# GpSimd takes the low halves of one projection, the second layer's S5 parameters are made earlier, and half of the LRU input product is done in split form

## What is computed

```python
h = rms_norm(x, norm_g)
p = h @ w_in                      # u_lru, u_s5, q/k/v of retention, nsa q, nsa k/v, gates, merges
y = [rg_lru(u_lru), s5(u_s5), retention(q, k, v), nsa(q, kv)]      # each 512 wide
merged = sum(sigmoid(merge_b) * ((silu(gate_b) * y_b) @ w_branch[b]) for b in 4 branches)
x = x + merged @ w_out
# S5: dt = exp(log_dt); a = exp(lam * dt) (complex); B and C are scaled by functions of a and lam
```

## Time and profile before

| | us |
|---|---|
| median of 3 runs | 751.04 |
| lowest and highest | 749.69, 751.25 |
| time of the profiled execution | 749.62 |
| its span, first to last instruction | 747.8 |
| TensorE busy | 734.8 |
| VectorE busy | 486.2 |
| ScalarE busy | 421.2 |
| GpSimd busy | 307.4 |

### The profile page before, as it was taken

How to read it: one execution, slowest core, us unless ns; L and a number is a source line. 1 busy time by engine, 2 the same in 40 slices (tenths; PEclk the granted TensorE clock), 3 DMA queues, 4 the chain that set the end, 5 groups by cost and what they waited for, 6 DMA issues and landing times.

```text
span 747.8 us, 14583 instructions
## 1 busy us (share of the span) xinstructions
PE 734.8 (98%) x6014; PEld 623.7 (83%) x6014; DVE 486.2 (65%) x786; ACT 421.2 (56%) x676; POOL 307.4 (41%) x135
## 2 busy tenths in 40 slices
PE   8999999999999999999989999999999999999996
PEld 7888898889888888878888878988898788888785
DVE  5989977675685634535688799767565947153344
ACT  7885635538464655544558664444476345655442
POOL 3000000035977976688100000000647979766750
PEclk9999999999999999999999999999999999999999
DMA  8669637553553655555545875665625456545541
GB/s 261 188 197 272 218 124 226 185 180 114 159 151 115 196 147 144 164 173 167 150 95 169 283 190 172 202 201 187 200 85 169 134 149 175 168 137 170 172 137 56
DMA packets 87009, 126.85 MB, mean 170 GB/s; under 512 B 22072, under 2 KB 32672, under 8 KB 86944
## 3 DMA queue, kind: packets, MB, share of 16 engines
q1 hardware_dynamic: 86624, 125.63, 55.9%
q10 hardware_dynamic: 320, 0.30, 0.1%
HBM read 124.86 MB, written 1.05 MB: 168 GB/s over the span
## 4 chain that ended last, share of the span: by engine, by line
PE 93%; DVE 3%; issue 2%; ACT 1%; DMA 0%; POOL 0%; SPq 0%; POOLq 0%; DVEq 0%; ACTq 0%
PE proj L1745 68%; PE M L1740 5%; PE proj L1782 4%; PE proj L1786 2%; PE proj L1813 2%; PE M L2140 2%; PE M L1942 1%; DVE sc L1556 1%; PE M L1953 1%; PE M L1910 1%; PE proj L1828 1%; PE proj L1844 1%; PE M L2114 1%; PE M L2017 1%; PE M L2109 1%
## 5 line engine op out<-in xcount | busy, mean ns | idle before, releaser
L698 POOL TENSOR_TENSOR w_lo<-raw,w_hi 128x1024 fp32r<-128x1024 f32 x112 | 291.4, 2633 | 391.8 <-ACT w_hi L720 368.7
L720 ACT ACTIVATE w_hi<-raw 128x1024 fp32r<-128x1024 f32 x200 | 206.5, 1054 | 108.8 <-PE proj L1745 64.8
L1745 PE MATMUL proj<-w_hi,h_hi 128*128 128x512 f32 x544 | 216.8, 399 | 0.0
L1745 PE MATMUL proj<-w_hi,h_lo 128*128 128x512 f32 x544 | 212.4, 390 | 0.0
L1745 PE MATMUL proj<-w_lo,h_hi 128*128 128x512 f32 x544 | 212.0, 390 | 0.0
L1745 PEld LDWEIGHTS proj<-w_hi,h_lo 128*128 128x128 f32 x544 | 102.1, 188 | 22.2 <-issue 0.5
L1745 PEld LDWEIGHTS proj<-w_hi,h_hi 128*128 128x128 f32 x544 | 102.2, 188 | 21.8 <-issue 0.9
L1745 PEld LDWEIGHTS proj<-w_lo,h_hi 128*128 128x128 f32 x544 | 102.3, 188 | 20.4 <-issue 0.5
L1329 DVE TENSOR_TENSOR w_lo<-raw,w_hi 128x1024 fp32r<-128x1024 f32 x80 | 95.0, 1221 | 27.0 <-ACT w_hi L720 19.5
L1745 PE MATMUL proj<-w_hi,ys_hi 128*128 128x512 f32 x128 | 51.0, 398 | 0.0
L1745 PE MATMUL proj<-w_hi,ys_lo 128*128 128x512 f32 x128 | 50.0, 391 | 0.0
(11 more groups left out here) (342 smaller groups left out, 1175.7 us busy)
## 6 DMA issues: line engine op xcount, KB each, us to landing
raw<-in_w_in SPq DMA_DIRECT2D x152, 512.0 KB, 4.3
raw<-in_w_branch SPq DMA_DIRECT2D x32, 512.0 KB, 4.0
raw<-in_w_out SPq DMA_DIRECT2D x16, 512.0 KB, 4.1
raw<-in_s_w_glu SPq DMA_DIRECT2D x8, 512.0 KB, 4.8
raw<-in_w_in SPq DMA_DIRECT2D x8, 256.0 KB, 3.0
merged<-in_nsa_ck_w SPq DMA_DIRECT2D x4, 512.0 KB, 6.9
mt<-in_nsa_ck_w SPq DMA_DIRECT2D x4, 512.0 KB, 8.9
merged<-in_nsa_cv_w SPq DMA_DIRECT2D x4, 512.0 KB, 4.6
```

Source lines behind the costliest of these rows:

```text
L698: nc.gpsimd.tensor_tensor(w_lo[:, slot(s, l), 0:n * w], raw[:, u % N_RAW, 0:n * w], w_hi[:, slot(s, l), 0:n * w].bitcast(f32), ALU.subtrac ...
L720: i = nc.scalar.activation(out_, in_, func, **kw)
L1745: last = mm(dst, left[i], right[j], start=start and n == 0, stop=stop and n == 2, skip_group_check=True)
```

## The change

Three things. (1) `nsa_kv` leaves `LO_ON_VECTOR`, so that GpSimd subtracts its four units in each layer. (2) Units 2 and 3 of `u_lru` are no longer native: ScalarE casts them after it has read the `cmp` chunk, VectorE subtracts them between `make_v(0)` and `make_v(1)`, and TensorE multiplies them in split form, as it does for `gate_lru`. The low part of `ret_v` unit 0 comes ahead of `make_v(1)` too. (3) In the first layer all five pieces of parameters of the second are made before the output projection's second half: `expand_dt`, `keep_vectors` and `_a` before `branch("nsa", 0)`, `_e` behind it, `_b`, `_c` and `_d` between `branch("nsa", 1)` and the lo part of the second half of `merged`. TensorE's `turn_vectors` moves from behind the second `blocks_T` to behind `branch_nsa_0`, and ScalarE's exponentials and sines move with it. The second layer no longer has `_c` and `_d` at its start.

```diff
-NATIVE = ("cmp", "u_lru")
+NATIVE_UNITS = [... "cmp" units 0 to 3, "u_lru" units 0 and 1]
-LO_ON_VECTOR = ("u_s5", "ret_v", "nsa_kv", ...
+LO_ON_VECTOR = ("u_s5", "u_lru", "ret_v", ...
...
                     run(bgate[:, :, :], cm[:, :, 256:CMP_W], ACT.Tanh, cmp_read, scale=0.5)
+                    cast_units(UNIT_END[CHUNK["u_lru"]])
                     keep_wT(0, 0)
...
                     cast_room("branch_nsa_0")
+                    if l + 1 < DEPTH:
+                        parameters_exp(l + 1)
...
                             cast_units(UNIT_END[CHUNK["branch_nsa_1"]] + N_SPLIT)
+                            if l + 1 < DEPTH:
+                                parameters_mag(l + 1)
+                                parameters_sin(l + 1)
...
                     make_v(0)
+                    split_lo("u_lru", 2, 3)
+                    split_lo("ret_v", 0)
                     make_v(1)
-                    split_lo("ret_v", 0, 1)
+                    split_lo("ret_v", 1)
...
-                    split_lo("nsa_kv", 0, 1)
                     scan_out(0)
-                    split_lo("nsa_kv", 2, 3)
...
                     lo_of_gated("nsa")
-                    branch("nsa", 0)
-
                     if l + 1 < DEPTH:
                         expand_dt(vector, l + 1)
+                        keep_vectors(vector, l + 1)
+                        parameters_a(l + 1)
+                    branch("nsa", 0)
+                    if l + 1 < DEPTH:
+                        parameters_e(l + 1)
                     for half in range(2):
                         if half:
                             branch("nsa", 1)
+                            if l + 1 < DEPTH:
+                                parameters_b(l + 1)
+                                parameters_c(l + 1)
+                                parameters_d(l + 1)
                         dve.wait_ge(mhi_done, half + 1)
...
                     chunk("branch_nsa_0")
-
+                    if l + 1 < DEPTH:
+                        pe.wait_ge(no_cmp, 1)
+                        turn_vectors(tensor, l + 1)
                     chunk("branch_nsa_1", 0)
                     pe.wait_ge(mt_free, 5)
+                    if l + 1 < DEPTH:
+                        Layer(tensor, l + 1).wait_ge(vec_ready, 1)
                     blocks_T(0, merged[:, 0]).then_inc(mT_done, 1)
...
-                    if l + 1 < DEPTH:
-                        turn_vectors(tensor, l + 1)
                     chunk("out_1a")
```

More of the change, by code:

```diff
@@ L69 @@
 N_SPLIT = 5
-NATIVE = ("cmp", "u_lru")
-SPLIT_UNITS = [u for u in range(NU) if CHUNKS[UNITS[u][0]][0] not in NATIVE]
-LO_ON_VECTOR = ("u_s5", "ret_v", "nsa_kv", "gate_s5", "gate_lru", "merge_s5_0", "merge_s5_1", "ret_q", "ret_k", "nsa_q",
+NATIVE_UNITS = [u for u in range(NU) if (CHUNKS[UNITS[u][0]][0], u - UNIT_END[UNITS[u][0] - 1]) in
+                [("cmp", n) for n in range(4)] + [("u_lru", n) for n in range(2)]]
+SPLIT_UNITS = [u for u in range(NU) if u not in NATIVE_UNITS]
+LO_ON_VECTOR = ("u_s5", "u_lru", "ret_v", "gate_s5", "gate_lru", "merge_s5_0", "merge_s5_1", "ret_q", "ret_k", "nsa_q",
                 "out_0b", "out_1b")
@@ L106 @@
     "dec_ready": 2, "dt_exp": 1, "dt_rows": 1, "evacuated0": 16, "evacuated1": 16, "gate_tanh": 2, "h_done": 2,
-    "hfull_done": 8, "hhi_done": 8, "hi_done": 100, "hidT_done": 2, "hid_arg": 1, "hid_ready": 1, "hid_tanh": 1,
+    "hfull_done": 8, "hhi_done": 8, "hi_done": 102, "hidT_done": 2, "hid_arg": 1, "hid_ready": 1, "hid_tanh": 1,
     "hid_tm_ready": 2, "hlo_done": 8, "kcT_done": 1, "kcT_ready": 1, "kc_ready": 1, "kern_ready": 2, "kp_done": 2,
-    "lam_abs": 1, "lam_exp": 1, "lo_done": 56, "lru_act": 16, "lru_m2": 1, "lru_mm": 1, "lru_sqrt": 1,
+    "lam_abs": 1, "lam_exp": 1, "lo_done": 60, "lru_act": 16, "lru_m2": 1, "lru_mm": 1, "lru_sqrt": 1,
     "mT_done": 2, "mag_arg": 1, "mag_exp": 1, "mhi_done": 2, "mlo_done": 2, "mt_free": 6, "nT_done": 2,
@@ L115 @@
     "v0_ready": 1, "v_ready": 2, "var": 2, "vbd_ready": 1, "vecT": 2, "vec_ready": 1, "vectors_loaded": 208,
-    "vk_ready": 2, "vlo_done": 44, "wT_done": 4, "wT_ready": 4, "w_ready": 2, "wbd_ready": 2, "wl_loaded": 64,
+    "vk_ready": 2, "vlo_done": 42, "wT_done": 4, "wT_ready": 4, "w_ready": 2, "wbd_ready": 2, "wl_loaded": 64,
     "xT_done": 4, "x_half": 3, "x_scaled": 4, "xc_ready": 1, "y_done": 2, "y_ready": 2, "yg_hi": 4, "yg_lo": 4,
@@ L1217, in _ @@
                         vector.wait_ge(const_loaded, 16)
-                    parameters_c(l)
-                    parameters_d(l)
+                        parameters_c(0)
+                        parameters_d(0)
                     v.memset(u_lru[:, :, 0:3], 0.0)
@@ L1674, in _ @@
                     lo_of_gated("nsa")
+                    if l + 1 < DEPTH:
+                        expand_dt(vector, l + 1)
+                        keep_vectors(vector, l + 1)
+                        parameters_a(l + 1)
                     branch("nsa", 0)
                     if l + 1 < DEPTH:
-                        expand_dt(vector, l + 1)
+                        parameters_e(l + 1)
                     for half in range(2):
@@ L1684, in _ @@
                                         flat(h_hi[:, 4 * half:4 * half + 4, :]).bitcast(f32), ALU.subtract).then_inc(mlo_done, 1)
-                    if l + 1 < DEPTH:
-                        split_lo("out_0b", 0)
-                        keep_vectors(vector, l + 1)
-                        split_lo("out_0b", 1)
-                        parameters_a(l + 1)
-                        parameters_e(l + 1)
-                    else:
-                        split_lo("out_0b", 0, 1)
+                    split_lo("out_0b", 0, 1)
                     split_lo("out_1b", 0, 1)
@@ L1706, in _ @@
                                            ALU.mult, ALU.add).then_inc(x_half, 1)
-                    if l + 1 < DEPTH:
-                        parameters_b(l + 1)
-                    else:
+                    if l + 1 == DEPTH:
                         vector.wait_ge(g_loaded, 16)
@@ L1762, in chunk @@
                             _, k0, nk, _ = UNITS[u]
-                            if name in NATIVE:
+                            if u in NATIVE_UNITS:
                                 pe.wait_ge(raw_loaded[u % N_RAW], raw_target[u])
@@ L1787, in chunk @@
                                                       start=st_, stop=sp_, skip_group_check=True)
-                                elif name in ("gate_s5", "gate_lru"):
+                                elif name in ("u_lru", "gate_s5", "gate_lru"):
                                     for m in range(4):
@@ L2197, in _ @@
                     if l + 1 < DEPTH:
-                        Layer(tensor, l + 1).wait_ge(vec_ready, 1)
                         for t in range(TT):
```

3 lines of the change are left out of this document (removed).

## The result

The changed kernel takes **758.94 us** (median of 4 runs, 758.83 to 759.29) against 750.41 us (749.69 to 751.25) for the kernel before on the same chip: a ratio of 1.0121, 95% interval 1.0109 to 1.0133. It is slower, as forecast, but by 8.5 us instead of 4.75, and lies 1.4 us above the range. (The forecast stood on 751.04 us, the median of the three runs of before that were there at the time; with a fourth run it is 750.41.) The profiled execution has a span of 757.0 us, 9.2 more than before.

The account below looks back on a forecast made before the run. TensorE's own list of work was taken to bound the kernel, any new VectorE lateness paid in full. -2.2 + 1.85 + 3.7 + 1.4 = +4.75 us on the median 751.04 gave 755.8 us; range 752.2 to 757.5.

Parts of the forecast that it names:

- Split half of `u_lru`: TensorE's list shortens 1.1 us a layer, 2.2 in all; a 1.85 us stop in layer one, none in layer two.
- Hand-over: End of layer one: `keep_vectors` and a held `_a` delay the pair; `blocks_T` 4.1 us late, 3.7 net of the turn.
- The clears: End of layer one: GpSimd's clears hold VectorE's `_b`, so `out_0b`'s low part is 1.4 us late.
- Rival (a): End of layer one: the clears do not hold VectorE; +3.35 us, 754.4; chance 0.21.
- (b): Hand-over: small one-input operations take no turns with GpSimd; +1.75 us, 753 to 754; chance 0.14.
- (c): Hand-over: no turns there as GpSimd is elsewhere, only the order counts; +0.35 us, 751.4; chance 0.08.
- (d): VectorE reaches `u_lru` in time, the end's hand-over hides, only TensorE's shorter list counts; -2.2 us, 748.9; chance 0.05.
- `nsa_kv` on GpSimd: Both layers: costed at nothing; VectorE's scans lose turns, with some 10 us until TensorE asks for them.
- Rival (e): GpSimd is late with `nsa_kv` or `ret_v` slips, 1 us a layer more; 757.8; chance 0.10.
- Behind the hand-over: From the first `blocks_T` to `out_0b`: `_b` ends at 362.6, `out_0b`'s low part is there at 369.3, 1.4 us late.

Follow-up runs that it names:

- f1: Kernel before with only the second layer's parameters made early, but `keep_vectors` and `_a` behind the first branch pair; 755.36 us, ratio 1.0076.
- e4: The changed kernel with `nsa_kv`'s subtractions back on VectorE, the two other parts kept; 757.63 us, ratio 1.0101.
- g2: The changed kernel with the update of the first half of `x` ahead of the next layer's two input low parts on VectorE; 757.07 us, ratio 1.0089.
- e2: Kernel before with only units 2 and 3 of `u_lru` split; 749.49 us, ratio 0.9999.
- e3: Kernel before with only `nsa_kv`'s subtractions moved to GpSimd; 750.96 us, ratio 1.0014.
- g1: Kernel before with `u_lru` units 2, 3 split, subtracted before `make_v(0)` in layer one, and `nsa_kv` unit 0's low part before the scans; 747.36 us, ratio 0.9961.
- g4: g1 with `nsa_kv`'s four subtractions a layer on GpSimd, none of them ahead of the scans on VectorE; 752.36 us, ratio 1.0035.
- g3: Kernel before with two unused copies of 1024 numbers from PSUM on VectorE ahead of the first branch pair in layer one; 752.38 us, ratio 1.0035.
- f4: Kernel before with three unused copies of 1024 numbers from PSUM on VectorE ahead of the first branch pair in layer one; 754.96 us, ratio 1.0081.
- e1: Kernel before with only the second layer's parameters made early; 756.96 us, ratio 1.0099.

## Why the prediction was right, and where it was wrong

**Split half of `u_lru`: right.** 5.94 us for 5.9. The start is 1.90 us behind that in the earlier trace rows, of which 0.11 come from the start of the program, for 1.85; the bracket shows 1.62 of it. Layer two has no stop. Net +0.72 and -1.16 us for +0.75 and -1.1.

**Hand-over: right in mechanism, 0.5 us too high.** One tiny operation of `_a` was held for a turn, 2.36 us where I had said 2.4. `blocks_T` came 3.69 late for 4.1, and 3.23 net of the turn for 3.7; the distance to `branch_nsa_0` is 6.43 for 6.8.

**The clears: right, though the gap is not to be seen in the changed kernel's own trace.** The clears hold `_b` (f1: 2.95 us, e4: 2.96, changed kernel: 1.73), but one operation and not two. The gap ahead of `out_0b` is 1.41 in e4 and 1.38 in g2. In the changed kernel's trace a lower clock stands in its place, which costs 1.57. Rival (a) falls, and so do (b) and (c), since the turns are all there, and (d).

**`nsa_kv` on GpSimd: wrong.** "I cost it at nothing", and "VectorE's scans run beside it and lose turns, with some 10 us until TensorE asks for them". The term that failed is this nothing. I did not count how many turns. By the rows it is 2.1 us at each of two scans, 2.0 at L1306 (0.68 before) and 2.0 at the additions of L1427 (3.70 for 1.65), 8.2 us against the 4.7 us of four subtractions taken away: VectorE is 3.3 us later at `keep_kernels(1)` in layer one (L1336 at 91.60 before, L1340 at 94.90 after), with a shift of TensorE of 0.83. Its slack there was 1.7 us, and TensorE waits 0.67 us at 95.62. In both layers together this is 0.53 + 1.86 = 2.4 us in the trace of the changed kernel (with the 0.3 that e2 and e4 show for part two alone), 1.15 by e3's median and 5.0 beside g1. The price depends on what else VectorE has to do: in e2 the second part's subtractions alone take 0.65 us of its slack ahead of `own_outputs(1)` in layer two (VectorE 1.65 us later than before, TensorE 1.00). Rival (e), with a chance of 0.10, had up to 1 us a layer and a slip of `ret_v`, which is there (+0.75 in layer two, and 1.44 us of wait in g4), but put it to GpSimd being late; it is VectorE that is held.

**Behind the hand-over: incomplete.** My working stopped at the low part of `out_0b`: "ends at 362.6, and the low part is there at 369.3". It is there at 370.3, about as said (with the 0.8 us shift of the first layer). What failed is that the sum ends there and puts what follows at nothing, without a reason. The lateness goes on, through the refill of its raw slots, to the cast and low part of the next layer's inputs, which VectorE takes ahead of the update of `x`. That is +1.45 us at the turn of `x`, undone by one move in g2.

**The clock: not in the sum.** No term had it. +0.91 us behind the turn of `x`, and +1.57 where I had 1.4 from another cause.

Together: 4.75 + 2.4 (`nsa_kv`) + 1.45 (turn of `x`) + 0.9 (clock) + 0.2 (1.57 for 1.4) - 0.5 (hand-over) = 9.2, the difference of the spans. By the medians it is 8.5. My range went wrong with the terms that I had at nothing, `nsa_kv`, the way on to the turn of `x`, and the clock: none had an upper bound in it that was worked out. The terms that I did work out came within 0.5 us of what they measured.

Two slips in the working change nothing in the sum. I read GpSimd's third subtraction in the earlier trace rows as about 1 us above its neighbours; that holds for the first (2.50 us), but the second took 3.38. And rival (d) is 748.8, not 748.9.

What stays open: why the granted clock falls behind some stops of 3.0 us and not behind others of the same length, and how much of it is in each median. It is not in the profiled runs alone. In g3 the four executions with a mean granted clock of 0.999 have spans of 750.0 to 750.7 us, the two at 0.996 and 0.994 have 752.1 and 753.0; f4's at 0.992 has 755.7 against 752.7 to 753.4 at 0.996 to 0.997. In e4 the profiled execution (0.997, 755.1) is the fastest, and the three others stand at 0.992 with 755.8 to 756.1. Where in those executions the clock was low is not recorded. Open too is the pause of 0.8 to 1.0 us in layer two of e3 and f1.

## What to carry to other kernels

When work is moved to GpSimd, count a hold of VectorE for each GpSimd instruction that runs beside its operations (here four, of 2.0 to 2.1 us); compare these holds less the work taken away (8.2 us less 4.7) with VectorE's slack at its next hand-over (here 1.7). When a hand-over comes late, follow the lateness through the buffers it frees and the loads that wait for them up to the next place where the engines meet. A shorter list of the engine that bounds the kernel is only worth its length if every low part behind it, which is now asked for earlier, is still in time: g1 needed one subtraction moved ahead of two scans to turn 0 into 2.7 us.

## What the runs showed of the hardware

- A clear by GpSimd, which reads nothing, holds a one-input operation of VectorE on 16 numbers until it ends: 2.95 us (f1) where it takes 0.17 alone.
- Of several tiny operations in a row, the one that comes when a GpSimd instruction has begun is held until that one ends, and those behind it take their usual time if GpSimd then has nothing more to run: in the changed kernel L1128 took 2.36 us and ended at 350.86, with GpSimd's third subtraction; its neighbours L1127 and L1129 took 0.16.
- Stops of 3.0 to 3.5 us of TensorE were followed by a granted clock of 0.50 in three executions of five, at a cost of 1.5 to 1.6 us. Behind the turn of `x` it fell after stops of 2.6 to 2.7 us (changed kernel, e4, f1; not after 2.48 in e1) and also after stops of 1.2 to 1.3 us in two executions of ten (e2, f2), at 0.9 to 1.3 us.
- Low clock and a later wait of the same engine overlap: where the next thing it waits for is set by another engine, what the clock costs is taken off that wait (1.57 us and no gap in the changed kernel; no low clock and a gap of 1.41 in e4).
